# Modulation sums of the first blocks on TensorE: weights in the array, the condition streamed

## The reference

```
c_act = jax.nn.silu(c)
mod = c_act @ w_ada[l] + b_ada[l]
sh1, sc1, g1, sh2, sc2, g2 = jnp.split(mod, N_MOD, axis=-1)
h = modulate(rms_norm(x, norm1_w[l]), sh1, sc1)       # h * (1 + sc1) + sh1
mix = hybrid_mixer(h, w_in[l], ...)
x = x + g1[:, None, :] * mix
```

## Time and profile before

| | us |
|---|---|
| median of 3 runs | 913.32 |
| lowest, highest | 912.99, 917.46 |
| the profiled execution | 921.88 |
| its span, first to last instruction | 920.1 |
| PE, DVE, ACT busy | 893.8, 667.6, 505.1 |
| first product matmul | 37.81 |

### The profile page before, as it was taken

How to read it: one execution, slowest core, us unless ns; L and a number is a source line. 1 busy time by engine, 2 the same in 40 slices (tenths; PEclk the granted TensorE clock), 3 DMA queues, 4 the chain that set the end, 5 groups by cost and what they waited for, 6 DMA issues and landing times.

```text
span 920.1 us, 18632 instructions
## 1 busy us (share of the span) xinstructions
PE 893.8 (97%) x8020; PEld 850.1 (92%) x8020; DVE 667.6 (73%) x1132; ACT 505.1 (55%) x814; POOL 65.8 (7%) x83
## 2 busy tenths in 40 slices
PE   5998999999999999999999999999999999999997
PEld 2798998999898999999999999999899999999997
DVE  4878767566978677677798775588665688778652
ACT  2489667454354627555354444466665576666442
POOL 0100201021001001020000000120000200000011
PEclk9999999999999999999999999999999999999999
DMA  8754233333767665465988889526331455555631
GB/s 335 279 191 162 102 129 104 128 138 109 259 232 247 209 229 179 165 217 179 288 326 295 287 287 255 218 96 226 138 138 53 177 184 192 190 192 178 223 126 46
DMA packets 27681, 177.31 MB, mean 193 GB/s; under 512 B 2864, under 2 KB 5680, under 8 KB 7504
## 3 DMA queue, kind: packets, MB, share of 16 engines
q1 hardware_dynamic: 27600, 176.13, 54.7%
HBM read 174.29 MB, written 1.84 MB: 191 GB/s over the span
## 4 chain that ended last, share of the span: by engine, by line
PE 82%; DVE 8%; ACT 6%; DMA 2%; issue 1%; DVEq 0%; SPq 0%; ACTq 0%
PE ps L1093 46%; PE ps L1099 22%; PE ps L1091 2%; DVE wl L1841 2%; DVE acc L1740 1%; ACT wh L1454 1%; PE ps L1138 1%; PE ps L1146 1%; PE ps L1232 1%; PE ps L1149 1%; PE ps L1097 1%; DMA raw<-in_ada_dram 1%; PE ps L1252 1%; PE ps L1303 1%; DMA raw<-in_w_sc_dram 1%
## 5 line engine op out<-in xcount | busy, mean ns | idle before, releaser
L1093 PE MATMUL ps<-HH,wh 128*128 128x256 f32 x1480 | 374.1, 288 | 0.7 <-DVE wl L1841 0.2
L1841 DVE TENSOR_TENSOR wl<-raw,wh 128x1024 fp32r<-128x1024 f32 x265 | 320.2, 1228 | 73.4 <-ACT wh L1454 72.8
L1093 PE MATMUL ps<-HH,wl 128*128 128x256 f32 x1480 | 361.0, 279 | 0.0
L1454 ACT ACTIVATE wh<-raw 128x1024 fp32r<-128x1024 f32 x265 | 273.8, 1043 | 142.5 <-PE ps L1099 112.9
L1093 PEld LDWEIGHTS ps<-HH,wh 128*128 128x128 f32 x1480 | 280.4, 189 | 9.8 <-issue 4.3
L1093 PEld LDWEIGHTS ps<-HH,wl 128*128 128x128 f32 x1480 | 279.8, 189 | 1.9 <-issue 1.9
L1099 PE MATMUL ps<-HL,wh 128*128 128x256 f32 x1480 | 229.1, 279 | 0.3 <-DVE HL L1786 0.3
L1099 PEld LDWEIGHTS ps<-HL,wh 128*128 128x128 f32 x1480 | 197.1, 189 | 0.6 <-DVE HL L1786 0.5
L1093 PE MATMUL ps<-FH,wh 128*128 128x256 f32 x352 | 85.9, 278 | 0.0
L1093 PE MATMUL ps<-FH,wl 128*128 128x256 f32 x352 | 85.9, 278 | 0.0
L1740 DVE SCALAR_TENSOR_TENSOR acc<-raw,silc,acc 128x512 f32<-128x512 f32 x101 | 76.3, 756 | 8.0 <-DMA raw<-in_ada_dram 4.9
(11 more groups left out here) (269 smaller groups left out, 1080.9 us busy)
## 6 DMA issues: line engine op xcount, KB each, us to landing
raw<-in_ada_dram SPq DMA_DIRECT2D x32, 1024.0 KB, 5.2
raw<-in_w_fi_dram SPq DMA_DIRECT2D x22, 1024.0 KB, 4.9
raw<-in_w_up_dram SPq DMA_DIRECT2D x22, 1024.0 KB, 4.8
raw<-in_w_rest_dram SPq DMA_DIRECT2D x20, 1024.0 KB, 4.8
raw<-in_w_in_dram SPq DMA_DIRECT2D x16, 1024.0 KB, 4.8
raw<-in_w_qkv_dram SPq DMA_DIRECT2D x12, 1024.0 KB, 4.8
raw<-in_w_o_dram SPq DMA_DIRECT2D x8, 1024.0 KB, 4.8
raw<-in_w_fo_dram SPq DMA_DIRECT2D x8, 1024.0 KB, 5.0
```

The costliest lines, as they stand in the source:

```text
L1093: e.matmul(o, w[:, k, 128 * t:128 * t + 128], x_hi[:, k0 + k, :], start=first and n + k == 0, **MM)
L1454: e.activation(whl[u % HALF][0][:, 0:n], raw[i % RAW][:, c:c + n], ACT.Copy).then_inc(*a_hi.up(u))
L1841: e.tensor_tensor(wl[:, 0:n], raw[i % RAW][:, c:c + n], wh[:, 0:n].bitcast(F32), ALU.subtract).then_inc(*v_lo.up(u))
```

## The change

All of blocks 0 and 1 goes to PE, and the operands change places: a piece of 128 x 128 of the weight is the stationary operand and the element column of silu(c) the streamed one, so each of 16 matmuls per item adds into one column of PSUM, and the result stands on the partitions at once. ACT's copy of the row and the turning matmuls (`ada_turn`) are gone. For blocks 2 and 3 a matmul with a column of ones as the streamed operand, on each 128 columns of `acc`, takes the place of transpose and reduce; blocks from 4 on are as before. The 16 fillers ahead of block 3 and the 10 ahead of the first product become 5 ahead of item (1,1) and 6.

```
-        ada_item(b, kp, rows=b == 0 or (b, kp) == (1, 0))
+        ada_item(b, kp, rows=b < 2)
...
-            if b == 1 or kp == 1:
-                tasks.append(ada_turn(b, rows_bank[0]))
+            if kp == 1:
+                emit("turn", b, 1, rows_bank[0], i)
+                misc.give(rows_bank[0], v_misc, "mod", b)
...
-    def ada_turn(b, bank):
-        slot, before = yield from take(acc)
-        emit("turn", b, 0, slot, bank, before)
-        misc.give(bank, a_misc, "row", b)
-        bank, before = yield from take(misc)
-        emit("turn", b, 1, slot, bank, before)
...
         for _ in range(LATER):
-            yield
-        while b == 1 and ("turn", 1, 1) not in made:
             yield
...
-            for _ in range(10):
+            for _ in range(6):
                 e.matmul(o[:, 0:128], ones, eye, start=True, **MM)
...
+                if (blk, kp) == (1, 1):
+                    for n in range(5):
+                        e.matmul(psum[b][:, 128:256], ones, eye, start=False, **MM)
...
                 for n in range(4):
-                    kt = 4 * kp + n
-                    ins = e.matmul(psum[b][0:1, :], silc[:, kt:kt + 1], raw[i % RAW][:, 512 * n:512 * n + 512],
-                                   start=kt == 0, **MM)
+                    for k in range(4):
+                        kt = 4 * kp + k
+                        at = 512 * k + 128 * n
+                        ins = e.matmul(psum[b][:, n:n + 1], raw[i % RAW][:, at:at + 128], silc[:, kt:kt + 1],
+                                       start=kt == 0 and n == 0, **MM)
...
-                if blk == 3:
-                    for _ in range(16):
-                        e.matmul(psum[b][:, 0:128], ones, eye, start=True, **MM)
                 v_misc.wait_ge(e, "ada", summed[blk][-1])
                 for n in range(4):
-                    ins = e.transpose(psum[b][:, 128 * n:128 * n + 128], accs[s][:, 128 * n:128 * n + 128], eye)
+                    part = accs[s][:, 128 * n:128 * n + 128]
+                    if blk < 4:
+                        ins = e.matmul(psum[b][:, n:n + 1], part, ones[:, 0:1], start=True, **MM)
+                    else:
+                        ins = e.transpose(psum[b][:, 128 * n:128 * n + 128], part, eye)
...
+        if b < 4:
+            e.tensor_tensor(col, psum[bank][:, 0:4], bias, ALU.add).then_inc(*v_misc.up("mod", b))
+            v_misc.at[("red", b)] = v_misc.at[("mod", b)]
+            return
```

More of the change, by code:

```diff
@@ L470, in ada @@
             tasks.append(ada_reduce(b, sums[b][0]))
-    def ada_turn(b, bank):
-        slot, before = yield from take(acc)
-        emit("turn", b, 0, slot, bank, before)
-        misc.give(bank, a_misc, "row", b)
-        bank, before = yield from take(misc)
-        emit("turn", b, 1, slot, bank, before)
-        acc.give(slot, p_misc, "turn", b)
-        misc.give(bank, v_misc, "turn", b)
     def ada_reduce(b, slot):
         for _ in range(LATER):
-            yield
-        while b == 1 and ("turn", 1, 1) not in made:
             yield
@@ L495, in mod @@
     def mod(b):
-        until(*((("turn", n, 1) if n == 0 else ("red", n, 1)) for n in (2 * b, 2 * b + 1)))
+        until(*((("turn", n, 1) if n < 2 else ("red", n, 1)) for n in (2 * b, 2 * b + 1)))
     part = []
@@ L1230, in tensor_engine @@
                 for n in range(4):
-                    kt = 4 * kp + n
-                    ins = e.matmul(psum[b][0:1, :], silc[:, kt:kt + 1], raw[i % RAW][:, 512 * n:512 * n + 512],
-                                   start=kt == 0, **MM)
-                ins.then_inc(*p_misc.up("rows", i))
[L1235 to L1243, removed]
+                    for k in range(4):
[3 more added lines that the diff above has]
+                                       start=kt == 0 and n == 0, **MM)
+                ins.then_inc(*p_misc.up("rows", i))
             elif kind == "red" and ev[2] == 0:
@@ L1469, in scalar_engine @@
                 e.activation(silc[:, :], v("c", 0, 8), ACT.Silu).then_inc(*a_misc.up("silc"))
[L1470 to L1474, removed]
             elif kind == "norm_sq":
@@ L1730, in dve_ada @@
         acc_ = accs[s][:, :]
-        begun = b != 1 and kp == 1
+        begun = kp == 1
         for n in range(4):
@@ L1747, in dve_reduce @@
         col = modc[:, 4 * b:4 * b + 4]
-        bias = col if b == 1 else v("b_ada", 4 * b, 4) if b < 12 else v("b_ada_f", 4 * (b - 12), 4)
+        bias = v("b_ada", 4 * b, 4) if b < 12 else v("b_ada_f", 4 * (b - 12), 4)
         p_misc.wait_ge(e, "red", b)
+        if b < 4:
+            e.tensor_tensor(col, psum[bank][:, 0:4], bias, ALU.add).then_inc(*v_misc.up("mod", b))
+            v_misc.at[("red", b)] = v_misc.at[("mod", b)]
+            return
         if previous is not None:
@@ L1754, in dve_reduce @@
         v_misc.wait_ge(e, "red", b)
-        if b == 1:
-            v_misc.wait_ge(e, "turn", 1)
         e.tensor_tensor(col, adr[:, :], bias, ALU.add).then_inc(*v_misc.up("mod", b))
@@ L1864, in vector_engine @@
                     e.memset(S["inv"][hi, :, lo], 0.0).then_inc(*v_misc.up("zero_inv"))
-            elif kind == "turn" and ev[2] == 1:
-                _, blk, _, s, b, _ = ev
-                p_misc.wait_ge(e, "turn", blk)
+            elif kind == "turn":
+                _, blk, _, b, i = ev
+                p_misc.wait_ge(e, "rows", i)
                 d_vec.wait_ge(e, "vec")
                 ins = e.tensor_tensor(modc[:, 4 * blk:4 * blk + 4], psum[b][:, 0:4], v("b_ada", 4 * blk, 4), ALU.add)
-                ins.then_inc(*v_misc.up(*(("mod", 0) if blk == 0 else ("turn", 1))))
-                if blk == 0:
-                    v_misc.at[("turn", 0)] = v_misc.at[("mod", 0)]
+                ins.then_inc(*v_misc.up("mod", blk))
             elif kind == "red" and ev[2] == 1:
```

## The result

| | before | after |
|---|---|---|
| median of 4 runs, us | 913.15 | 934.96 |
| lowest, highest | 911.15, 917.46 | 925.97, 936.11 |
| the profiled execution | 921.88 | 925.97 |
| its span | 920.1 | 924.2 |
| first product matmul | 37.81 | 45.05 |

The ratio is 1.0211 (95%: 1.0138 to 1.0284). The change makes the kernel slower, and the prediction (914.6, range 908 to 922) was wrong. The sum of its rival (a), 924.0, is nearest and still too low. Two further comparisons gave 1.0167 (1.0134 to 1.0200) and 1.0144 (1.0083 to 1.0205): the loss is clear in all three, its size between some 8 and 26 us. The ratios are of several runs on each side and are not exactly those of the medians.

The account below looks back on a forecast made before the run. PE, busy 97% of the span, was taken as the bound, so only unhidden time counts. From the profiled 921.9 us, -1.4 (begin) and +2.7 (heads) gave 923.2, or 914.6 beside the median of 913.32; range 908 to 922.

Parts of the forecast that it names:

- rival (a): Begin: one-column blocks run at the low clock, first product 8.0 us later, total 924.0 us; chance 0.20.
- The columns: Begin: a column block of 32 records takes 3.7 us at full pace, so PE gains nothing per block.
- -1.4: Begin: the first product starts at 36.4 instead of 37.81 us, 1.4 us gained; bounds 0 and 3.0.
- The begin at full clock: Begin: w1c written at 25.6 us, item (1,1) landed at 30.3, PE standing 2 us for it, first product at 36.4.
- The wait for KT: Head 0, step 0, near 78 us: PE stands 1.5 us until DVE has written the normalised KT.
- The wait of head 1 for qg: Head 1, step 1, from 89.05 us: PE stands 3.8 us until ACT has done qg at 92.8.
- The low stretch of 6.8 us: Behind head 1's wait for qg: clock low for 6.8 us, a loss of 3.4 us (bounds 1.7 and 3.4).
- The sum, +2.7: Stage of the heads: 0.7 us less before the clock, 3.4 us lost to it, so 2.7 us slower.
- the re-dealt waits, taken as 0: Later PE waits in the stage of the heads, re-dealt by the shift: taken as 0, bounds -4 and +4 us.
- two stretches at the low clock: Profiled execution before: stretches of 6.8 and 3.4 us, costing about 3.4 and 1.7 us, which other runs may lack.
- The carry-over: Profile to median: differences, not levels, are carried over, so 923.2 us by the profile became 914.6 beside 913.32.

Follow-up runs that it names:

- second profile of before: The kernel before run again with no edit, for a second profile: span 909.6 us, time of that execution 911.35 us.
- experiment 2: The changed kernel with each condition column and the ones column streamed 96 times instead of once: 921.06 us, ratio 1.0090 to the kernel before; also called the wide version.
- three profiles after: The changed kernel profiled three times with no edit, in the first comparison and two repeats: spans 924.2, 928.0 and 921.8 us.
- steps moved alone: The kernel before with the tick counter put 2 on behind the begin, so every head step stands two tiles earlier: 916.59 us, ratio 1.0044.
- wide, restored: The changed kernel with columns streamed 96 times and the tick counter put 1 on, restoring the head steps: 915.45 us, ratio 0.9991 to the kernel before.
- experiment 4: The changed kernel with the tick counter put 1 on behind the begin, so head steps stand as in the kernel before: 922.05 us, ratio 1.0102.
- experiments 1, 3, 4 and 11: 1 and 11: changed kernel again, no edit, 1.0167 and 1.0144; 3: kernel before, tick counter 2 on, 1.0044; 4: changed kernel, counter 1 on, 1.0102.

## Why the prediction was wrong, by its own steps

**The columns: the step that failed.** "A column block is 32 x 0.115 = 3.7 us" holds at the upper clock (3.63), and the prediction then took that clock for the whole begin. It rested on 1.05 us of such records that had left the pace as it was the earlier trace rows, a stretch too short to bear it, and gave the other outcome 0.20. Every step of rival (a) came, each a little earlier than worked out:

| | rival (a) | measured |
|---|---|---|
| block (0,0) | 7.4 us, to 16.6 | 6.99, to 16.0 |
| norm ends | 21.9 | 21.0 |
| w1c | 28.8 | 27.72 |
| block (1,1) ends | 41.2 | 40.8 |
| first product | 45.8 | 45.05 |

That the last rows agree so well is in part luck, for two errors cancel: the sum priced a record at the low clock at 0.23 us, where 0.21 was measured (6.83 us for 32), and it left out the five fillers ahead of (1,1), which take 2.3 us.

In place of -1.4 the begin cost 7.2 in the first pair of profiles, and 7.8 to 10.9 against the second profile of before. The Trainium skill ("TensorE: Matmul & The Clock Gate", Part 1, What's actually happening) says that a monitor sets the gate by how busy the array has been, and is silent on weight loads with one streamed column. By experiment 2 they do not bear the busy clock, although PE's records leave no gap; on this the trace says more than the page.

**The begin at full clock** was sized well, as the wide version shows: w1c 25.05 for 25.6, item (1,1) at 30.65 for 30.3, PE standing 2.77 us for 2. That PE would keep its clock behind this wait was wrong: the block at half pace is 3.2 of the 3.4 us between 36.4 and the 39.8 measured.

**The heads.** The wait for KT (1.5 predicted) is 1.63, 1.62 and 1.59 us in the three profiles after, and 1.43 with the steps moved alone. The wait of head 1 for qg (3.8) is 2.24, 3.86 and 2.30, and 2.25 alone. The chain through ACT and DVE is as told; what the prediction lacked is a low stretch of 3.4 us behind the wait for KT, which stands in the first and third profile after and with the steps moved alone. PE then comes late to qg and waits 2.2 to 2.3 us; in the second profile after, without that stretch, it waits 3.86. The low stretch of 6.8 us that I put behind the wait for qg is 3.4 us in the first two profiles after and missing in the third. Nor does the length of a wait tell what the clock does: behind a wait of 1.58 us at 282 us the clock of before stayed at 1.00.

The sum, +2.7, is 4.0 (2.5 to 5.6) alone, and some 4 to 6 on top of the slow begin. It is near for other reasons than mine: moved alone, the two named waits make 3.7 us in place of 2.8, 0.9 more, where I had 5.3 in place of 2.6. The missing terms are the re-dealt waits, taken as 0 (inv 1.1 and y 0.5 us where the old order has none before 175 us, and 4.2 in place of 3.6 behind it), and the 1.8 us of slow pace in the 400 records behind the stage: seven profiles show it (47.1 for 45.3), all six with the steps moved among them, and one with them restored (wide, restored), so it is no sure mark of the order.

**From profile to median.** I put the 8.6 us by which the profiled execution exceeds the median down to two stretches at the low clock (5.1 us). The larger part was the slow pace of the last 1480 records, 6.4 us at a granted clock of 1.00, and record durations of 281 instead of 276 ns would have told. The carry-over itself was sound as a rule, but it hid that the profile of before is no fair partner for that of after: the second pair of spans, 909.6 and 928.0, shows 18.4 where the first shows 4.1. By parts these are 10.9 at the first product, 6.2 to record 4680, 1.8 of pace, -0.4 behind it, 0 at the end.

**The range** ended at 922 because it left out "the worst of (a)". Rival (a), 8.0 for the begin and 2.7 for the heads on 913.3, is 924.0; the later comparisons say 928 and 929, the first 935. Its two terms were 8.0 and 2.7 where 9 (experiment 4) and 4 to 6 (experiments 1, 3, 4 and 11) were measured.

## What to carry to other kernels

A busy PE row says nothing of its clock: compare the time of the same number of records in two places, and where a rewrite cuts the columns streamed per weight load, as here, run that piece at length before trusting the upper clock, and price the lower one for all that follows until it is back. Where side work is placed by a counter, check what a change far ahead does to that counter; here one number restored the order and some 4 to 6 us. Before carrying a difference of two profiles to medians, check that the unchanged tail of both ran at the same pace.

## What the runs showed that I had not expected

- Streaming 96 columns for each load of 128 fp32 weights costs the same as streaming one (3.71 and 3.63 us for 32 records), and the granted clock, once risen, stayed at 1.00 until PE had to wait; with one column 20 us of PE work without a gap, most of it such records, ran at 0.50. The Trainium skill ("TensorE: Matmul & The Clock Gate", Part 4) says that transposes do not count as busy in the same way; these are plain matmuls, and no run here has transposes at length.
- At a granted clock of 1.00 the fp32 products run at one of two paces, a matmul every 113.3 or every 117.8 ns, and keep it for stretches of tens of us, in the first profile of before for over 200 us up to the end. The granted clock does not show it, and no run here tells what sets it.
- Item (1,1), late by 2.8 us, cost 3.2 us more through the clock: the wait's price was double its length.
